# Differential mixer of a hybrid attention layer: the reciprocal sums of a block in four sets of columns in place of two

## The reference, cut to what matters

```
for blk in range(s // Q_BLOCK):                       # 8 blocks of 128 queries
    qs = blk * Q_BLOCK; qe = qs + Q_BLOCK
    sc = einsum('bqhmd,bkhmd->bhmqk', q[:, qs:qe], k[:, :qe]) * HEAD_DIM ** -0.5
    sc = where(allowed, sc + bias, NEG_INF)           # m = 0, 1: two score maps a head
    pr = softmax(sc, axis=-1)
    a = pr[:, :, 0] - lam * pr[:, :, 1]
    outs.append(einsum('bhqk,bkhe->bqhe', a, v[:, :qe]))
o = rms_norm(concatenate(outs), subln_g) * (1.0 - lambda_init)
```

## Time and profile before

| what | us |
|---|---|
| median of 3 runs | 1322.36 |
| lowest, highest | 1321.7, 1324.58 |
| the profiled execution, own time | 1325.6 |
| its span, first to last instruction | 1323.8 |
| TensorE busy in the span | 1229.1 (93%) |
| VectorE busy | 878.5 (66%) |
| ScalarE busy | 518.3 (39%) |
| GpSimd busy | 322.6 (24%) |

### The profile page before, as it was taken

One profiled execution on the slowest core, in us unless ns is written; L12 is line 12 of the kernel. 1 busy time (PEld: TensorE's weight loads), 2 busy tenths in 40 slices (PEclk: granted clock), 3 DMA queues, 4 the chain that ended last, 5 costly groups with the idle time before them and its releaser, 6 DMA issues.

```text
span 1323.8 us, 16977 instructions
## 1 busy us (share of the span) xinstructions
PE 1229.1 (93%) x6103; PEld 1004.9 (76%) x6103; DVE 878.5 (66%) x1466; ACT 518.3 (39%) x1042; POOL 322.6 (24%) x335
## 2 busy tenths in 40 slices
PE   4999999898776499999999999999999999999997
PEld 3997787676655388788888888888888768888885
DVE  3423786665666346687777877877777998773442
ACT  3422664544545212343333333333344434652231
POOL 0000000343443211223223313323213890000000
PEclk9999999999789799999999999999999999999999
DMA  6363232011640431123323233333288534620101
GB/s 197 78 97 82 54 83 73 28 41 60 157 161 1 112 95 49 65 88 119 104 96 121 89 93 97 120 103 96 89 298 312 184 99 116 222 88 21 44 32 48
DMA packets 128669, 136.08 MB, mean 103 GB/s; under 512 B 15570, under 2 KB 93130, under 8 KB 128522
## 3 DMA queue, kind: packets, MB, share of 16 engines
q1 hardware_dynamic: 128586, 135.00, 34.0%
HBM read 96.77 MB, written 37.22 MB: 101 GB/s over the span
## 4 chain that ended last, share of the span: by engine, by line
PE 54%; DVE 8%; issue 3%; DMA 2%; SPq 1%; ACT 0%; POOL 0%; POOLq 0%; DVEq 0%; ACTq 0%
PE ps L1679 53%; DVE wbuf L1180 4%; DVE more L1180 1%; DMA raw<-u_ops 1%; DVE h L1605 1%; PE ps L1689 1%; DMA raw<-in_w_out 1%; PE ps L1885 0%; SPq L479 0%; DVE conv L1402 0%; ACT wbuf L799 0%; DVE a_t L1180 0%; PE ps L2039 0%; DVE small L1304 0%; POOL stat L678 0%
## 5 line engine op out<-in xcount | busy, mean ns | idle before, releaser
L1679 PE MATMUL ps<-act_t,wbuf 128*128 128x512 f32 x1200 | 290.3, 398 | 2.9 <-DVE wbuf L1180 2.9
L1679 PEld LDWEIGHTS ps<-act_t,wbuf 128*128 128x128 f32 x1200 | 226.9, 189 | 57.8 <-issue 3.3
L1679 PE MATMUL ps<-wbuf 128*128 128x512 f32 x912 | 217.1, 392 | 2.0 <-DVE wbuf L1180 1.9
L1679 PEld LDWEIGHTS ps<-wbuf 128*128 128x128 f32 x912 | 170.0, 188 | 40.8 <-DVE wbuf L1180 4.1
L1679 PE MATMUL ps<-act_t,wq 128*128 128x512 f32 x624 | 158.2, 407 | 3.7 <-DVE wq L1182 2.8
L1679 PEld LDWEIGHTS ps<-act_t,wq 128*128 128x128 f32 x624 | 116.7, 192 | 34.2 <-issue 7.7
L1180 DVE TENSOR_TENSOR wbuf<-raw,wbuf 128x512 fp32r<-128x512 f32 (+1 forms) x107 | 106.1, 992 | 20.6 <-ACT wbuf L799 20.1
L799 ACT ACTIVATE wbuf<-raw 128x512 fp32r<-128x512 f32 (+1 forms) x107 | 69.2, 649 | 94.2 <-PE ps L1679 70.5
L678 POOL TENSOR_TENSOR stat<-stat 128x1 f32<-128x1 f32 x32 | 17.6, 549 | 360.8 <-DVE stat L1189 360.8
L1679 PE MATMUL ps<-hx,wbuf 128*128 128x512 f32 x408 | 96.2, 391 | 0.0
L1679 PEld LDWEIGHTS ps<-hx,wbuf 128*128 128x128 f32 x408 | 76.5, 188 | 16.6
(11 more groups left out here) (197 smaller groups left out, 2065.9 us busy)
## 6 DMA issues: line engine op xcount, KB each, us to landing
u_ops<-wbuf_f SPq DMA_DIRECT2D x77, 256.0 KB, 2.2
raw<-u_ops SPq DMA_DIRECT2D x77, 256.0 KB, 2.7
raw<-in_w_ffn_in SPq DMA_DIRECT2D x33, 512.0 KB, 3.9
g_ffn<-in_w_ffn_in SPq DMA_DIRECT2D x11, 512.0 KB, 4.0
act_f<-in_w_ffn_out SPq DMA_DIRECT2D x21, 256.0 KB, 3.6
w_raw<-in_w_in SPq DMA_DIRECT2D x10, 512.0 KB, 4.5
wbuf_f<-in_w_ffn_out SPq DMA_DIRECT2D x18, 256.0 KB, 6.8
x_in<-in_x SPq DMA_DIRECT2D x8, 512.0 KB, 3.7
```

The source lines that it names most:

```text
L1679: return nc.tensor.matmul(dst, lhs, rhs, start=start, stop=stop)
```

## The change

The two reciprocals and the factor of block m go to columns 4 * (m mod 4) to 4 * (m mod 4) + 2, four sets in columns 0 to 15. VectorE's wait becomes one for the scaled output of block m-4. ScalarE reads its scale from the new column.

```
-                col = 32 + 16 * (m % 2) + 12
+                col = 4 * (m % 4)
                 nc.scalar.activation(o_sb[:, :, :], ps[:, 7, 0:2 * P].rearrange(...), ACT.Copy,
                                      scale=small[:, col:col + 1]).then_inc(S.b_part, 1)
...
             dve.wait_ge(S.b_exp, 2 * m + 2)
-            if m >= 2:
-                dve.wait_ge(S.b_part, m - 1)
-            link(nc.vector.reciprocal(small[:, o + 12:o + 14], small[:, o + 8:o + 10]))
-            link(nc.vector.scalar_tensor_tensor(out=small[:, o + 14:o + 15], in0=small[:, o + 13:o + 14],
+            c = 4 * (m % 4)
+            if m >= 4:
+                dve.wait_ge(S.b_part, m - 3)
+            link(nc.vector.reciprocal(small[:, c:c + 2], small[:, o + 8:o + 10]))
+            link(nc.vector.scalar_tensor_tensor(out=small[:, c + 2:c + 3], in0=small[:, c + 1:c + 2],
                                                 scalar=lamt[:, 5:6], in1=small[:, o + 8:o + 9], op0=ALU.mult,
                                                 op1=ALU.mult))
             nc.vector.scalar_tensor_tensor(out=e_t[:, q, 0, 0:w], in0=e_t[:, q, 1, 0:w],
-                                           scalar=small[:, o + 14:o + 15], in1=e_t[:, q, 0, 0:w],
+                                           scalar=small[:, c + 2:c + 3], in1=e_t[:, q, 0, 0:w],
                                            op0=ALU.mult, op1=ALU.add).then_inc(S.b_diff, 1)
```

## The result

The changed kernel took 1290.45 us (median of 4, 1289.78 to 1295.41) against 1323.47 us (median of 4) before: 33.0 us less by the medians, ratio 0.976 with a 95% interval of 0.9739 to 0.9782 (by the ratio 31.8 us). Forecast were 1297 us, range 1289 to 1309. The profiled execution took 1291.0 us with a span of 1289.2 us, 34.6 us less than the span before. Two executions of all that follow are not counted, one of before (3087 us, beside runs 5 and 10 to 12) and one of run 12 (4227 us), each more than twice as long as every other one.

A forecast was written before the change was run, and what follows sets the result against it. TensorE, busy 93% of the span, bounds the kernel, in a closed loop with VectorE and ScalarE. Stall 22.1, shorter product 1.7 and clock 1.7 make 25.5 us: 1300.1 us profiled, 1297 as median, range 1289 to 1309.

The forecast's parts named there:

- main forecast: Whole kernel: 22 to 29 us gained, a median of 1293 to 1300.5 us, chance 0.56.
- rival (b): Clock stays up throughout the mixer, later falls go too, second term in full: 30 us gained, 1292 us, chance 0.17.
- (c): A later transfer or another wait on the same edge absorbs all, or another semaphore released the reciprocal: 1322 us, chance 0.05.
- (d): Wide product holds GpSimd back until y comes after TensorE's work: 13 us slower, 1335 us, chance 0.04.
- The stall and its cause: Reciprocal opening each mixer block's difference waits for ScalarE's scaled output, 45.7 us in 26 of 32 blocks; this should go.
- The stretches that follow from the stall alone: Later mixer iterations: 18 to 20 gain 1.6 us, 21 and 22 0, 23 and 24 3.2, 28 to 32 7.2.
- the shorter product: VectorE's wide product, moved away from GpSimd's product, saves 0.3 us in blocks of 768 columns; 1.7 us in all.
- The gain is the smaller of the stall that goes and TensorE's gap before the next scores: Iterations with a TensorE half-unit, n under 20: 4.1 us in 3 to 7, 5.0 us in 10 to 15.
- the high half takes nothing back: In n = 30 ScalarE's high half ends at 412.73, before the difference's new end at 413.52, so costs nothing.
- n = 8 and 9 are full on TensorE: 0: In these iterations TensorE's own work fills the period, so the stall that goes gains 0 us.
- The clock, 1.7 us of 3.4 at 262 and 317 us: TensorE's clock falls twice after idle gaps, each costing 1.7 us; one of the two was taken as going.
- The rule on GpSimd and VectorE: Wide product excludes GpSimd's power and scaling: y of n = 30 some 0.9 us later, near 415.1, costing 0 there.

The follow-up runs named there:

- run 5: Kernel before, plus unread matmuls keeping TensorE busy in gaps of iterations 8, 16, 24 and 32: 1322.18 us, ratio 0.9984.
- run 10: Changed kernel with TensorE's transposes of y moved behind the products of the block: 1291.19 us, ratio 0.9748.
- run 11: Changed kernel with ScalarE's output-weight copies in iterations 20, 21, 25 and 26 put ahead of the exponentials: 1287.10 us, ratio 0.9717.
- run 12: Changed kernel with y's transposes behind the products and ScalarE's output-weight copies ahead of the exponentials: 1288.87 us (median of 3), ratio 0.9733.
- run 1: Changed kernel with its four sets of columns, but VectorE's old wait for block m-2: 1326.19 us, ratio 1.0005.
- run 6: Changed kernel with the old wait put back for blocks 7, 8, 15 and 16 (iterations 8, 9, 16, 17): 1293.97 us, ratio 0.9775.
- run 7: Kernel before in its waits, in four column sets, with the new wait for blocks 7, 8, 15 and 16 only: 1321.44 us, ratio 0.9979.
- run 8: Kernel before with the new wait for blocks 7, 8, 15, 16 only, plus unread matmuls in iterations 8 and 16: 1320.02 us, ratio 0.9972.
- run 9: Changed kernel measured once more, nothing altered: 1291.66 us, ratio 0.9758.

## Why the prediction was right, and where it was off

*The number:* the measured 1290.45 us lies in the stated range, 1.45 us above its lower end, and outside the main forecast of 1293 to 1300.5 us. Inside the mixer 33.7 us were gained where 25.5 were forecast. Of the 8.2 us that are missing, 3.3 lie in iterations 8, 9, 16 and 17, 2.5 are later falls of the clock, some 1.7 are the cap by TensorE's gap, and the rest is small. What happened is closest to rival (b), 1292 us, which had a chance of 0.17: both falls at 262 and 317 us went, and so did the later ones where they cost time. The clock did not stay up throughout, as (b) has it, but where it is low now little or nothing is lost. Nothing came of (c) and (d). It was the range and not the central sum that held the result.

*The stall and its cause:* right. The row of 45.7 us is gone, and with the old wait alone put back it is there (run 1). In n = 30 the reciprocal moved as worked out.

*The stretches that follow from the stall alone:* right in size. 18 to 20, 21 and 22, 23 and 24, and 28 to 31 gained 11.4 us where 10.4 were forecast; the shorter product explains most of the difference (iterations 22 to 24 and 30 to 32 have the wide blocks). The sign that was set for 28 to 31, 1.3 to 1.8 us each, came out as 1.26, 1.38, 1.77 and 1.77.

*"The gain is the smaller of the stall that goes and TensorE's gap before the next scores":* wrong as a rule. By stall I mean, as the prediction does, the reciprocal's delay behind the exponentials and VectorE's own work. The forecast was 1.8 us too low in iterations 3 to 7 and 0.9 in 10 to 15. About 0.5 us of each is the shorter product, which the prediction counted as its second term; the rest is the cap. The whole stalls, 5.05 and 5.6 us, with the product's 0.5, come within 0.4 us of the 5.9 and 5.9 measured. The clearest case is iteration 3: in after TensorE's gap is used up, but the exponentials still moved by 1.26 us, as the stall of 1.22 says and not the gap of 0.42. The scores of iteration 4 start late, 0.84 us after the exponentials, and it does not matter: VectorE is not there before 232.67. Iteration 4 of after:

```profile
229.45 0.19 ACT L878 ACTIVATION_READ_ACCUMULATOR e_t<-ps,small 128x1 f32 x1
230.48 1.26 PE L1680 MATMUL ps<-wq 64*128 64x512 f32 x12
...
232.67 0.55 DVE L1305 TENSOR_REDUCE small<-ps 128x1 f32<-128x384 f32 x1
```

But the whole stall is not the rule either. In iteration 11 the stall was 1.13 us, the gap 0.67, and 0.81 was gained: VectorE's low half of `a_t` now waits 0.33 us for ScalarE's high half, which had waited for TensorE's transposes. The prediction had tested this wait at n = 30 alone ("the high half takes nothing back"). And in iterations 9, 17 and 25, in which TensorE makes the products of a block of 1024 columns, the stalls were 2.9, 3.2 and 4.0 us and 1.4, 1.3 and 2.0 us were gained.

```profile
271.90 0.28 ACT L799 ACTIVATE mst<-ps 128x128 fp32r<-128x128 f32 x1 [0.49 <-PE ps L1848]
...
272.56 0.42 DVE L1180 TENSOR_TENSOR a_t<-ps,a_t 128x256 fp32r<-128x256 f32 x1 [0.33 <-ACT a_t L799]
```

*"n = 8 and 9 are full on TensorE: 0", and the same for 16 and 17:* the largest error. The four iterations gained 5.0 us; the forecast had 0 for the stall and 1.7 for the clock there. TensorE was full only at 1.2 GHz: at the upper clock it stands idle for VectorE (run 5), and the stall put back costs 2.3 us a pair (run 6). Runs 5, 7 and 8 show both bounds: over three iterations 0.1 to 0.2 us for each alone and 1.7 for both. The change removes the gap that lets the clock fall and the stall that lies behind it.

*The clock, 1.7 us of 3.4 at 262 and 317 us:* the fall and its cause were read rightly, since both falls went with the gap, but not what they are worth. By run 5 those two falls cost 0.3 us as long as the stall is there, the later ones, which I left to the range, 0.9 at 25 and 1.6 at the end. With the stall gone they cost 1.5 us each (run 8 against run 7), close to the 1.7 of the prediction. The later falls account for the last stretch (3.4 for 1.6) and for much of iteration 25, which gained the whole 2.0 us of 25 to 27 where 0.95 were forecast. There the prediction also misread the trace: 25 has no weight split (these are in 21, 22, 26 and 27) but the longest stall of the loop:

```profile
382.39 0.17 DVE L1287 RECIPROCAL small<-small 128x2 f32<-128x2 f32 x1 [4.14 <-ACT o_sb L954]
```

*The shorter product:* right in size, 1.7 forecast. That only one-column operations of GpSimd would run beside it is not so everywhere: in iterations 6, 8, 14 and 16 its scaling (L700) does, and is the one held up. By shape the means fell from 1243, 1346 and 1372 ns to 1019, 1150 and 1285 for 768, 896 and 1024 columns, four of each, 2.0 us of VectorE's busy time in all.

```profile
L697 POOL TENSOR_TENSOR stat<-stat 128x1 f32<-128x1 f32 x32 | 27.1, 848 | 2.7
...
L1292 DVE SCALAR_TENSOR_TENSOR e_t<-e_t,small 128x1024 f32<-128x1024 f32 x4 | 5.1, 1285 | 0.1
L1292 DVE SCALAR_TENSOR_TENSOR e_t<-e_t,small 128x896 f32<-128x896 f32 x4 | 4.6, 1150 | 0.1
L1292 DVE SCALAR_TENSOR_TENSOR e_t<-e_t,small 128x768 f32<-128x768 f32 x4 | 4.1, 1019 | 0.1
```

*The rule on GpSimd and VectorE:* borne out in after, and free of cost as forecast. GpSimd's power, 0.57 us before, took 0.85 on the mean and 1.28 in n = 30, and y ended 3.2 us behind the exponentials (3.4 forecast by the rule). One detail is open: in n = 30 of before it was the wide product that took longer (1.32 us), though its row starts 0.05 us ahead of GpSimd's L703, which kept its 0.46 us. By the prediction's own sign of being wrong, y as releaser of TensorE's transposes, this part came near: there are 5 such waits in after, 2.4 us. Moving them away brought nothing (run 10).

*The rest moves with the mixer's end:* right, 34.2 us at its end, 34.6 in the span.

## What to carry to other kernels

Where an engine waits for the release of a small buffer in every iteration of a closed loop, one more copy of the buffer is worth up to the sum of the stalls (here 34 us were gained, clock and shorter product included, from 45.7 us of idle time). Count each whole at first, then ask in each iteration what the next releaser takes back; a gap of another engine is no cap by itself. When an engine looks full, ask at which clock: a stretch that is full at 1.2 GHz can hide a stall that comes out once the clock stays up, and then either cure alone shows little. After such a change look at the same place for the next releaser: here four weight copies in a late slot held another 3 to 5 us.

## What the runs showed of the hardware

A one-column GpSimd power (L697) takes 0.57 us alone and up to 1.55 us beside a VectorE product that reads two wide operands from on-chip memory; the longest ones stand beside the widest products.

The places of the low clock inside the mixer agree to 0.5 us in two profiled executions of after (after and run 9). That is no rule for this kernel: over the 44 counted executions of before in the three series the mean granted clock goes from 0.975 to 0.983, and the time goes with it. The median is 1325.6 us for the 23 executions with 0.977 or less and 1322.8 us for the 12 with 0.981 or more. So the number of falls changes from one execution to the next, and is worth some 3 us. The profile of before (0.976) is one with many falls. A difference of a microsecond or two in this kernel may be the clock's, far from the edit: run 7 differs only in iterations 8, 9, 16 and 17, and its profile has 1.6 us at the mixer's end from a fall that is not there. Its ten executions have a median clock of 0.984 against 0.977 for before beside them, so the edit may have moved the falls as well, and one profile cannot part the two.
